# The level loop and the order of the grams in a chunked recurrence on one Trainium2 core

## The chip, the cores and the metric

The kernel runs on one core of a Trainium2 chip. The metric is the device time of one execution in microseconds (us). The kernel before took 4756.89 us in the median of three executions (4755.41 to 4758.74).

## The reference

Two blocks of layers follow each other; each has two layers. A layer of the first block mixes three kinds of heads over 256 context tokens and 1024 latent tokens: six heads of an RWKV-7 recurrence in both directions, six heads of grouped attention and four heads of windowed attention. The change lies in the recurrence alone. Per head, the state S is 64x64 and goes over the tokens one by one, forwards and backwards:

```python
def _rwkv7_step(S, inp):
    r, w, k, v, kk, b = inp
    sa = jnp.einsum('bhvk,bhk->bhv', S, kk)
    S = S * w[:, :, None, :] - sa[..., None] * b[:, :, None, :] + v[..., None] * k[:, :, None, :]
    return S, jnp.einsum('bhvk,bhk->bhv', S, r)
```

The backward direction runs the same step with the tokens reversed, and the outputs of both directions are added. Everything is in float32.

## The kernel before, in words

`rwkv_core` (from line 1606) runs the recurrence once per layer of the first block, so twice. It doesn't go token by token: the 1280 tokens are NB = 10 blocks of 128 tokens, each of two chunks c of 64, and the state is carried from chunk to chunk. The six heads are NP = 3 pairs g, each with two heads h, and two directions d; q = 2d + h counts the four of a pair. Most products are 64x64x64, one in a quarter of the systolic array: `half[0]` and `half[1]` are the lower and the upper 64 partitions, of the operands (a row half of the array) and of the result (a column half).

A block goes through these steps for each pair. TensorE's step is named first, then who takes the result from PSUM:

- `grams(b, g)` (line 1732): products of the loaded arrays of a chunk, masked by VectorE (`masked`, 2007) into G. They are made a block ahead, in the tail of block b - 1. The first array's gram is made in two products of 64 columns, since its two halves go to different column halves; the second's in one of 128. So a pair takes 24 products.
- `turned` (1748): eight transposes of loaded arrays, taken by ScalarE (X and V, 1967, 1968) and VectorE (2016).
- GpSimd masks the gram to the start matrix U0 and to the level matrices ML (2091, 2099); `start_t` (1765) makes the 64x64 inverse's start TU and its transpose; `bv` (1783) makes one more product.
- `state(b - 1, i)` (1882): the state's step for the block before, products at 1896 and 1904, additions at 2051 and 2056.
- Levels 1 to 5 double the size of the solved diagonal pieces: `level_w` (1797), copied by ScalarE to Ws (1980), then `level_d` (1816), which VectorE subtracts from both forms of TU in one instruction (2023). Levels 1 to 4 are four turns of a loop on TensorE, `pe.Fori(0, NL - 1)` at 1931. Level 5 is written out behind it: `level_w(b, NL, g)`, and `last_d` (1830) with half as many products, since only one form of TU is needed from there; VectorE subtracts it in two instructions of 64 partitions a pair (2027).
- `solve` (1843) multiplies TU with X; ScalarE takes the result to TX (1984). `outputs` (1854) makes four matrices a pair from TX, G and V, which VectorE adds and stores in QY and MN (2039, 2041). `state` needs them.

All orders are written by hand and every engine runs its own list; counters (semaphores) tie them together. TensorE's tail of a block is, before the change: loop, grams 0, W 0, W 1, grams 1, last_d 0, W 2, last_d 1, last_d 2, grams 2, solve 0, solve 1, outputs 0, solve 2, outputs 1, outputs 2 (lines 1940 to 1958). VectorE's: masks 0 and 1, the last level, mask 2, outputs 0, 1, 2. PSUM has eight banks, and the lists `d_at` to `state_at` (1668 to 1677) say which step writes which; a wait in `grams`, `turned`, `last_d` or `outputs` is for the step that had those banks before.

SP's queue (1690 to 1723) loads block b + 1 when the outputs of block b - 1 have been taken, and then stores the outputs of block b - 1. A load is six transfers of 384 KB (`rk_in`, one a pair and direction: 128 partitions, six arrays, 128 tokens, so runs of 512 bytes) and two of 192 KB for V. The first block's load stands first in the queue, six small constants behind it, the second block's load behind those. TensorE, VectorE and GpSimd all wait for the constants before they begin (1729, 2004, 2087).

The loop's body and the rest of TensorE's program are instructions read from memory; the profile shows their packets as the queue "q8 instruction".

Of the kernel before, what the change touches and what calls it, by code (L numbers as in the profile page):

```python
# [26 lines left out]
P = 128  # L27
# [6 lines left out]
HD = 64  # L34
# [1571 lines left out]
def rwkv_core(core):  # L1606
# [13 lines left out]
    d_in, v_in = [core.landing(f"rk_d{g}_loaded", per=2) for g in range(NP)], core.landing("rk_v_loaded", per=2)  # L1620
# [16 lines left out]
    with ExitStack() as s:  # L1637
# [32 lines left out]
        def w_at(g, last):  # L1670

            return bank[2 + g][:, 0:256] if g < 2 else bank[2][:, 0:256] if last else bank[0][:, 256:512]

        last_at, solve_at, bv_at = (bank[4], bank[5], bank[0]), (bank[2], bank[3], bank[2]), (bank[6], bank[7], bank[6])
        turned_at, start_at = (pair_at(0), pair_at(4), pair_at(0)), (by_chunk(2), by_chunk(6), by_chunk(2))
        gram_at, outputs_at = (pair_at(6), pair_at(0), pair_at(6)), (pair_at(0), pair_at(4), pair_at(6))
# [10 lines left out]
        with nc.Block() as block:  # L1687

            @block.sync
            def _(sp):  # L1690
                def load(b):
                    u, blk = b % 2, (b, back(b))
                    for g in range(NP):
                        for d in range(2):
                            sp.dma_start(D[:, u, g, d, 0:NA, :], T["CHK"][g * 2 + d, :, :, blk[d] * P:(blk[d] + 1) * P]
                                         .rearrange("w p t -> p w t")).then_inc(d_in[g].on(u), 16)
                        if g == 0:
                            for d in range(2):
                                sp.dma_start(VI[:, u, d, :, :], T["VT"][:, blk[d] * P:(blk[d] + 1) * P]
                                             .rearrange("(g p) t -> p g t", p=P)).then_inc(v_in.on(u), 16)  # L1700
# [25 lines left out]
            def _(pe):  # L1726
# [5 lines left out]
                def grams(b, g):  # L1732
# [5 lines left out]
                    elif b:  # L1738
                        pe.wait_ge(dl.sem, dl.nth(number(b - 1, NL - 1, 1 + g) + 1))
                    for d in range(2):  # L1740
                        for x, arr, a0, n in ((0, A_BH, A_KT, 1), (1, A_BH, A_RT, 1), (2, A_KH, A_KT, 2)):
                            for c, h in tiles:
                                rows, tok = half[h], half[c]
                                o = gram_at[g][h][half[1 - c if x == 0 else c], d * 256 + x * CH:d * 256 + (x + n) * CH]
                                ins = nc.tensor.matmul(o, D[rows, u, g, d, arr, tok], D[rows, u, g, d, a0:a0 + n, tok], start=True, stop=True)
                    ins.then_inc(pg.sem, 1)

                def turned(b, g):
# [3 lines left out]
                    if g < 2:  # L1752
                        after(pe, dq, NP * (b - 1) + g + 1)
# [29 lines left out]
                def bv(b, g):  # L1783
# [6 lines left out]
                    for q in range(4):  # L1790
                        d, h = q // 2, q % 2
                        for c in range(2):
                            ins = nc.tensor.matmul(bv_at[g][half[c], q * CH:(q + 1) * CH], G[half[c], u, g, d, h, 2, :],
# [1981 lines left out]
```

## Time and profile before

| | us |
|---|---|
| median of three runs | 4756.89 (4755.41 to 4758.74) |
| the profiled execution's own time | 4744.87 |
| its span (first to last instruction) | 4743.1 |
| TensorE busy, 86% of the span | 4102.1 |
| VectorE busy, 58% | 2756.3 |
| ScalarE busy, 33% | 1549.2 |
| GpSimd busy, 32% | 1498.3 |
| recurrence, first layer (from 556 to 978) | 422 |
| recurrence, second layer (from 2056 to 2475) | 419 |

PE is TensorE, DVE is VectorE, ACT is ScalarE, POOL is GpSimd, SP is SyncE. A float32 product of TensorE appears as two matmul records with a weight load each, so 24 products are 48 records; a transpose is one record. The brackets at the end of a timeline line give the time for which the engine stood just before, and what released it; "issue" means that it waited for nothing that the profile shows. Times in a timeline are from the start of the span.

### The profile page before, as it was taken

The page shows a single profiled execution, that of the slowest core. Times are in us where ns is not written, and L with a number is a line of the kernel's source. Part 1 is how long each engine was busy: PE and PEld are TensorE (multiplying, and loading weights), DVE is VectorE, ACT ScalarE, POOL GpSimd, SP SyncE. Part 2 cuts the span into 40 slices and gives each one's busy share as a digit, 9 for nine tenths or more (in the row PEclk, how much of TensorE's full clock was granted, in tenths as well). Part 3 has the DMA queues.
Part 4 walks back from the last instruction along what each step waited for, and adds up shares of the span by engine and source line. Part 5 has one row for each costly group of instructions (what it writes and reads, how often), then busy time and mean ns, then how long its engine had stood idle before and what let it go on. Part 6 is the DMA issues. An engine that isn't in the chain of part 4 may idle for free. (4 is left out here: it accounts for less than half of the span.)

```text
span 4743.1 us, 105248 instructions
## 1 busy us (share of the span) xinstructions
PE 4102.1 (86%) x43986; PEld 3151.5 (66%) x43986; DVE 2756.3 (58%) x4726; ACT 1549.2 (33%) x2721; POOL 1498.3 (32%) x1210
## 2 busy tenths in 40 slices
PE   6999888869989799888886999599679889978898
PEld 4878688836657587678874667488436677853566
DVE  3465455556657357545556665755657656557565
ACT  1333232325542133222224552200356420025542
POOL 2233143411004323324432013655132145514213
PEclk8999999979999899899998999699899999989899
DMA  6455533261235545643324134433312443340324
GB/s 195 154 176 190 167 83 83 60 219 33 62 93 173 156 152 202 201 118 83 83 79 123 46 78 168 149 111 104 122 35 66 126 163 100 104 142 7 83 64 175
DMA packets 502686, 560.45 MB, mean 118 GB/s; under 512 B 97532, under 2 KB 397084, under 8 KB 500180
## 3 DMA queue, kind: packets, MB, share of 16 engines
q1 hardware_dynamic: 374676, 475.93, 32.2%
q10 hardware_dynamic: 127616, 78.95, 5.7%
q8 instruction: 287, 4.70, 0.4%
q14 instruction: 107, 0.88, 0.1%
HBM read 366.75 MB, written 192.23 MB: 118 GB/s over the span
## 5 line engine op out<-in xcount | busy, mean ns | idle before, releaser
L1096 PE MATMUL pr_acc<-hH,pr_wh 128*128 128x512 f32 (+1 forms) x1288 | 482.4, 375 | 0.0
L1097 PE MATMUL pr_acc<-hL,pr_wh 128*128 128x512 f32 (+1 forms) x1288 | 466.1, 362 | 0.0
L1098 PE MATMUL pr_acc<-hH,pr_wl 128*128 128x512 f32 (+1 forms) x1288 | 465.6, 361 | 0.0
L2660 ACT ACTIVATE an_p<-an_p,an_stat 128x1280 f32<-128x1280 f32 (+5 forms) x372 | 339.7, 914 | 162.0 <-DVE an_stat L2738 156.5
L2600 PE MATMUL an_t<-ident,an_p 128*128 128x128 f32 x2152 | 318.5, 282 | 40.5 <-ACT an_pT L2667 28.1
L2600 PEld LDWEIGHTS an_t<-ident,an_p 128*128 128x128 f32 x2152 | 235.8, 141 | 164.1 <-issue 68.0
L2693 POOL TENSOR_TENSOR an_kl<-an_k,an_kh 128x1280 fp32r<-128x1280 f32 (+3 forms) x36 | 78.5, 2181 | 833.6 <-DVE an_qh L2718 833.6
L2734 DVE CUSTOM_DVE_ANT_0 an_p<-an_s,an_mask 128x256 f32<-128x256 f32 (+8 forms) x308 | 274.8, 892 | 99.5 <-PE an_s L2583 67.1
L2091 POOL TENSOR_TENSOR rk_ml<-rk_g,rk_lmask 128x256 f32<-128x256 f32 x300 | 210.7, 729 | 357.7 <-PE rk_ps L1812 357.0
L1465 POOL TENSOR_TENSOR sp_sl<-sp_w,sp_sh 128x512 fp32r<-128x512 f32 x172 | 246.0, 1437 | 196.4 <-DVE sp_sh L1540 177.9
L2625 PE MATMUL an_oacc<-an_pT,an_v 128*64 128x512 f32 (+3 forms) x1224 | 297.9, 561 | 4.0 <-DVE an_pT L2745 1.9
L1374 PE MATMUL sp_acc<-sp_ch,sp_sh 128*128 128x512 f32 x728 | 285.4, 392 | 7.6 <-POOL sp_sl L1465 7.6
L1140 POOL TENSOR_TENSOR pr_wl<-pr_w,pr_wh 128x1024 fp32r<-128x1024 f32 x58 | 142.7, 2461 | 472.2 <-DVE pr_wh L1160 472.2
L1376 PE MATMUL sp_acc<-sp_ch,sp_sl 128*128 128x512 f32 x728 | 284.8, 391 | 0.0
L1375 PE MATMUL sp_acc<-sp_cl,sp_sh 128*128 128x512 f32 x728 | 284.8, 391 | 0.0
L1096 PEld LDWEIGHTS pr_acc<-hH,pr_wh 128*128 128x128 f32 x1288 | 245.4, 191 | 58.0 <-issue 20.7
L2667 ACT COPY an_pT<-an_t 128x512 f32<-128x512 f32 (+3 forms) x356 | 186.0, 540 | 294.5 <-PE an_t L2600 293.6
L1097 PEld LDWEIGHTS pr_acc<-hL,pr_wh 128*128 128x128 f32 x1288 | 245.2, 190 | 37.8 <-issue 1.0
L1098 PEld LDWEIGHTS pr_acc<-hH,pr_wl 128*128 128x128 f32 x1288 | 244.8, 190 | 38.2
L2745 DVE COPY an_pT<-an_t 128x512 f32<-128x512 f32 (+3 forms) x256 | 155.6, 615 | 178.4 <-PE an_t L2600 175.7
L2023 DVE TENSOR_TENSOR rk_tu<-rk_tu,rk_ps 128x512 f32<-128x512 f32 x240 | 151.7, 683 | 183.6 <-PE rk_ps L1826 183.5
L2582 PE MATMUL an_s<-an_kh,an_qh 128*128 128x256 f32 (+2 forms) x564 | 198.3, 364 | 22.5 <-POOL an_qh L2697 13.5
(386 smaller groups left out, 10011.3 us busy)
## 6 DMA issues: line engine op xcount, KB each, us to landing
CHK<-ri_out SPq DMA_DIRECT2D x24, 1920.0 KB, 8.0
rk_in<-CHK SPq DMA_DIRECT2D x120, 384.0 KB, 6.5
pr_w<-in_w_in ACTq DMA_DIRECT2D x58, 512.0 KB, 3.9
UT<-pr_out SPq DMA_DIRECT2D x45, 640.0 KB, 4.3
sp_w<-in_w_in ACTq DMA_DIRECT2D x50, 512.0 KB, 5.1
U<-sp_c SPq DMA_DIRECT2D x100, 256.0 KB, 2.0
mod_w<-in_w_mod SPq DMA_DIRECT2D x16, 1024.0 KB, 7.9
mo_w<-in_w_out SPq DMA_DIRECT2D x16, 1024.0 KB, 10.2
```

The costliest lines, as they stand in the source:

```text
L1096: nc.tensor.matmul(out, wh[:, u, k, 0:m], hi, start=(k == 0), stop=False)
L1097: nc.tensor.matmul(out, wh[:, u, k, 0:m], lo, start=False, stop=False)
L1098: ins = nc.tensor.matmul(out, wl[:, u, k, 0:m], hi, start=False, stop=(k == KT - 1))
L1374: nc.tensor.matmul(to, sH[:, a, k, :], cH[:, i, k, :], start=(k == 0), stop=False)
L1375: nc.tensor.matmul(to, sH[:, a, k, :], cL[:, i, k, :], start=False, stop=False)
L1376: ins = nc.tensor.matmul(to, sL[:, a, k, :], cH[:, i, k, :], start=False, stop=(k == H - 1))
L1465: g.tensor_tensor(sL[:, slot(q, i)], weight(q, i), sH[:, slot(q, i)], ALU.subtract).then_inc(w_lo.sem, 1)
L2091: return nc.gpsimd.tensor_tensor(out, G[:, b % 2, g, :, :, 0, :], lm[:, :, lv:lv + 1, :].to_broadcast([P, 2, 2, CH]), ALU.mult)
L2600: ins = nc.tensor.transpose(bank[:, j * P:(j + 1) * P], Pm[:, n % NPM, j, col:col + P], ident[:])
L2625: ins = nc.tensor.matmul(O[half * HD:(half + 1) * HD, cs], V[:, c % 2, blocks[n][k], :], PT[:, buffer(n, k), cs], start=(p == 0), stop=(p ...
L2660: nc.scalar.activation(row, row, ACT.Exp, bias=stat[:, n % NPM, j, 1:2], scale=heads[groups[n][0]].scale, accum_out=total[:, n % 4, j:j + ...
L2734: V_.tensor_tensor_reduce(out=Pm[:, n % NPM, j, 0:width], in0=scores_at(m, width), in1=extra, scale=1.0, scalar=-3.0e38, op0=ALU.add, op1= ...
```

## The change

Four things change, all in `rwkv_core`.

1. Level 5 becomes a fifth turn of TensorE's loop, like the others, and `last_d` goes. VectorE subtracts it in one instruction a pair instead of two.
2. The order of the tail is new. TensorE: loop, solve 0, solve 1, grams 0, solve 2, outputs 0, grams 1, grams 2, outputs 1, outputs 2. VectorE: last level, mask 0, outputs 0, mask 1, mask 2, outputs 1, outputs 2. Banks and waits follow: outputs 0 use banks 4 and 5, outputs 1 use banks 0 and 1 and wait for mask 1, outputs 2 wait for mask 2; the next block's first transposes wait for outputs 1 instead of outputs 0, its second for outputs 0.
3. The first array's gram is one product of 128 columns, so a pair takes 16 products. All grams now lie in the other chunk's half of the partitions.
4. For that, the arrays that meet the grams later are loaded with their chunks exchanged. A load of a pair and direction is four transfers instead of one: two of two whole arrays, and two that bring half of the tokens of two arrays, in runs of 256 bytes. V comes in four transfers instead of two, also in runs of 256 bytes. A block's load is 28 transfers instead of 8.

```diff
@@ loads
-                            sp.dma_start(D[:, u, g, d, 0:NA, :], T["CHK"][g * 2 + d, :, :, blk[d] * P:(blk[d] + 1) * P]
-                                         .rearrange("w p t -> p w t")).then_inc(d_in[g].on(u), 16)
+                            src = T["CHK"][g * 2 + d, :, :, blk[d] * P:(blk[d] + 1) * P].rearrange("w p t -> p w t")
+                            for a in (A_BH, A_KT):
+                                sp.dma_start(D[:, u, g, d, a:a + 2, :], src[:, a:a + 2, :]).then_inc(d_in[g].on(u), 16)
+                            for c in range(2):
+                                sp.dma_start(D[:, u, g, d, A_BE:A_BE + 2, half[1 - c]], src[:, A_BE:A_BE + 2, half[c]]) \
+                                    .then_inc(d_in[g].on(u), 16)
                         if g == 0:
                             for d in range(2):
-                                sp.dma_start(VI[:, u, d, :, :], T["VT"][:, blk[d] * P:(blk[d] + 1) * P]
-                                             .rearrange("(g p) t -> p g t", p=P)).then_inc(v_in.on(u), 16)
+                                for c in range(2):
+                                    t0 = blk[d] * P + c * CH
+                                    sp.dma_start(VI[:, u, d, :, half[1 - c]], T["VT"][:, t0:t0 + CH].rearrange("(g p) t -> p g t", p=P)) \
+                                        .then_inc(v_in.on(u), 16)
@@ grams
-                        for x, arr, a0, n in ((0, A_BH, A_KT, 1), (1, A_BH, A_RT, 1), (2, A_KH, A_KT, 2)):
+                        for x, arr in ((0, A_BH), (2, A_KH)):
                             for c, h in tiles:
                                 rows, tok = half[h], half[c]
-                                o = gram_at[g][h][half[1 - c if x == 0 else c], d * 256 + x * CH:d * 256 + (x + n) * CH]
-                                ins = nc.tensor.matmul(o, D[rows, u, g, d, arr, tok], D[rows, u, g, d, a0:a0 + n, tok], start=True, stop=True)
+                                o = gram_at[g][h][half[1 - c], d * 256 + x * CH:d * 256 + (x + 2) * CH]
+                                ins = nc.tensor.matmul(o, D[rows, u, g, d, arr, tok], D[rows, u, g, d, A_KT:A_KT + 2, tok], start=True, stop=True)
@@ TensorE, tail of a block
-                    with pe.Fori(0, NL - 1) as i:
+                    with pe.Fori(0, NL) as i:
...
+                    solve(b, 0)
+                    solve(b, 1)
                     if more:
                         grams(b + 1, 0)
-                    level_w(b, NL, 0)
-                    level_w(b, NL, 1)
+                    solve(b, 2)
+                    outputs(b, 0)
                     if more:
                         grams(b + 1, 1)
-                    last_d(b, 0)
-                    level_w(b, NL, 2)
-                    last_d(b, 1)
-                    last_d(b, 2)
-                    if more:
                         grams(b + 1, 2)
-
-                    solve(b, 0)
-                    solve(b, 1)
-                    outputs(b, 0)
-                    solve(b, 2)
                     outputs(b, 1)
                     outputs(b, 2)
@@ VectorE
-                    for lv in range(1, NL):
+                    for lv in range(1, NLEV):
...
                     if more:
                         masked(b + 1, 0)
+                    outputs(b, 0)
+                    if more:
                         masked(b + 1, 1)
-                    level(b, NL, 0)
-                    level(b, NL, 1)
-                    level(b, NL, 2)
-                    if more:
                         masked(b + 1, 2)
-                    for g in range(NP):
-                        outputs(b, g)
+                    outputs(b, 1)
+                    outputs(b, 2)
```

In `bv`, `solve` and `outputs` the halves of the operands or of the result are exchanged to match; their numbers and shapes of products stay.

## Rows read from the trace of the kernel before

**Rows 1.** Windows, first recurrence: length; busy PE, PEld, DVE, ACT, POOL; PEclk, DMA share, GB/s.

```profile
556.00:978.00 422.00, 362.67 (x13700) 341.70 (x13700) 226.49 (x433) 121.80 (x300) 167.41 (x250) 0.97 0.31 79
```

**Rows 2.** Timeline of TensorE, a block's tail: start, us, engine, line, operation, count [idle].

```profile
757.89 1.13 PE L1745 MATMUL rk_ps<-rk_in 64*64 64x64 f32 x48 [0.59 <-DVE rk_tu L2023]
...
763.76 0.49 PE L1850 MATMUL rk_ps<-rk_x,rk_tu 64*64 64x128 f32 x5
...
765.52 0.45 PE L1866 MATMUL rk_ps<-rk_g,rk_tx 64*64 64x128 f32 x8
...
766.94 0.94 PE L1850 MATMUL rk_ps<-rk_x,rk_tu 64*64 64x128 f32 x12
...
771.48 0.44 PE L1760 MATMUL rk_ps<-ident,rk_in 128*128 128x128 f32 x2
```

**Rows 3.** Timeline of VectorE in the same tail.

```profile
759.11 1.29 DVE L2010 TENSOR_TENSOR rk_g<-rk_ps,rk_mask 128x512 f32<-128x512 f32 x2 [0.77 <-PE rk_ps L1745]
...
762.14 2.61 DVE L2027 TENSOR_TENSOR rk_tu<-rk_tu,rk_ps 64x256 f32<-64x256 f32 x6
...
767.28 0.43 DVE L2039 TENSOR_TENSOR rk_qy<-rk_ps,rk_in 128x256 f32<-128x256 f32 x1 [1.21 <-PE rk_ps L1878]
...
768.28 0.41 DVE L2041 TENSOR_TENSOR rk_mn<-rk_ps,rk_dg 128x256 f32<-128x256 f32 x1
```

**Rows 4.** Timeline of TensorE, third and fourth turn of the loop.

```profile
751.02 1.56 PE L1812 MATMUL rk_ps<-rk_tu,rk_ml 64*64 64x64 f32 x46 [0.27 <-issue]
...
754.29 1.56 PE L1812 MATMUL rk_ps<-rk_tu,rk_ml 64*64 64x64 f32 x46 [0.26 <-issue]
```

**Rows 5.** Timeline of TensorE in a layer's last block: fourth turn, first solve.

```profile
956.01 1.56 PE L1812 MATMUL rk_ps<-rk_tu,rk_ml 64*64 64x64 f32 x46 [0.26 <-issue]
...
962.12 0.61 PE L1850 MATMUL rk_ps<-rk_x,rk_tu 64*64 64x128 f32 x8
```

**Rows 6.** Timeline of TensorE, pauses of one block before and during the load.

```profile
723.65 0.27 PE L1869 MATMUL rk_ps<-rk_g,rk_tx 64*64 64x64 f32 x1 [0.23 <-issue]
...
727.07 0.27 PE L1866 MATMUL rk_ps<-rk_g,rk_tx 64*64 64x128 f32 x1 [0.39 <-issue]
...
736.05 0.38 PE L1896 MATMUL rk_ps<-rk_h,rk_mn 64*64 64x64 f32 x5 [0.72 <-issue]
...
742.38 2.47 PE L1812 MATMUL rk_ps<-rk_tu,rk_ml 64*64 64x64 f32 x46 [2.45 <-issue]
```

**Rows 7.** DMA queues: packets, MB, share, from 715 to 731, 731 to 744, 1244 to 1248.

```profile
q8 instruction: 4, 0.07, 1.7%
...
q1 hardware_dynamic: 6280, 3.14, 89.0%
q8 instruction: 2, 0.03, 1.0%
...
DMA packets 84, 0.02 MB, mean 5 GB/s; under 512 B 83, under 2 KB 83, under 8 KB 84
q1 hardware_dynamic: 84, 0.02, 2.3%
```

**Rows 8.** Windows, as rows 1, the microsecond after the longest pause.

```profile
743.00:744.00 1.00, 1.00 (x24) 1.00 (x22) 0.00 (x0) 0.37 (x1) 0.67 (x1) 0.50 0.22 62
```

**Rows 9.** Timelines of SP's queue and of TensorE at the start of a layer.

```profile
556.47 0.96 SPq L1695 DMA_DIRECT2D rk_in<-CHK  x2
...
563.03 1.28 SPq L1709 DMA_DIRECT2D rk_pair<-in_pair  x1
564.35 0.43 SPq L1711 DMA_DIRECT2D rk_mask<-in_mask_gram  x1
...
570.35 4.95 PE L1745 MATMUL rk_ps<-rk_in 64*64 64x64 f32 x128 [6.67 <-issue]
```

**Rows 10.** Timeline of SP's queue, the load inside a block.

```profile
730.76 0.95 SPq L1695 DMA_DIRECT2D rk_in<-CHK  x2
...
732.87 5.94 SPq L1695 DMA_DIRECT2D rk_in<-CHK  x4
```

More of the change, by code:

```diff
@@ L1619, in rwkv_core @@
     PER = NL * NP
-    d_in, v_in = [core.landing(f"rk_d{g}_loaded", per=2) for g in range(NP)], core.landing("rk_v_loaded", per=2)
+    d_in, v_in = [core.landing(f"rk_d{g}_loaded", per=8) for g in range(NP)], core.landing("rk_v_loaded", per=4)
     stored = core.landing("rk_y_stored", per=2)
@@ L1752, in turned @@
                     if g < 2:
-                        after(pe, dq, NP * (b - 1) + g + 1)
+                        after(pe, dq, NP * (b - 1) + 2 - g)
                     else:
@@ L1801, in level_w @@
                     pe.wait_ge(dl.sem, dl.nth(k - NP + 1))
-                    last = isinstance(lv, int)
-                    if g == 2 and not last:
+                    if g == 2:
                         after(pe, dh, 2 * b)
                         after(pe, dy, 2 * b)
-                    if not last:
-                        pe.sem_inc(turn.sem, 1)
+                    pe.sem_inc(turn.sem, 1)
                     for q in range(4):
@@ L1811, in level_w @@
                             far = half[1 - c]
-                            ins = nc.tensor.matmul(w_at(g, last)[half[c], q * CH:(q + 1) * CH], ML[far, g, d, h, :], TU[far, g, c, q, :],
+                            ins = nc.tensor.matmul(w_at[g][half[c], q * CH:(q + 1) * CH], ML[far, g, d, h, :], TU[far, g, c, q, :],
                                                    start=True, stop=True)
@@ L1828, in level_d @@
                     ins.then_inc(pd.sem, 1)
-                def last_d(b, g):
-                    k = number(b, NL, g)
-                    pe.wait_ge(aw.sem, aw.nth(k + 1))
-                    if g == 2 and b + 1 < NB:
-                        pe.wait_ge(dm.sem, dm.nth(NP * (b + 1) + 2))
-                    elif g == 2:
-                        pe.wait_ge(dl.sem, dl.nth(number(b, NL - 1, 2) + 1))
-                    for q in range(4):
-                        for c in range(2):
-                            ins = nc.tensor.matmul(last_at[g][half[c], q * CH:(q + 1) * CH], Ws[half[c], g, q, :], TU[half[c], g, c, q, :],
-                                                   start=True, stop=True)
-                    ins.then_inc(pd.sem, 1)
                 def solve(b, g):
```

45 lines of the change are left out of this document (20 added, 25 removed).

## The prediction

> **What bounds the kernel now.** The page has TensorE busiest, and its chain says little here, so I went by stage. The changed code is the recurrence, which runs once in each of two layers; the first run takes about 422 us, TensorE is busy in 362.67 us of that and VectorE in 226.49 [rows 1]. So what counts is TensorE's own order of work plus every place where it stands. The timeline of one block's tail shows them. From the first gram of the next block to the first transpose it takes 771.48 - 757.89 = 13.59 us; grams of one pair take 0.93 us (0.89 us in the shape after the change, below), solves of two pairs 765.52 - 763.76 = 1.76, so 0.88 each, and the outputs of one pair 766.94 - 765.52 = 1.42 [rows 2]. VectorE's part of it: two masks 1.29 us, six half subtractions 2.61, and the four additions of one pair 1.41, from 767.28 to 768.69 [rows 3]. A turn of the level loop takes 754.29 - 751.02 = 3.27 us [rows 4].
>
> Two other things bound it. TensorE's instructions come in packets of 16 KB on a queue of their own. Between loads four came in 16 us; while the next block was loading only two came in 13 us [rows 7]. The pauses marked "issue" fall in step: 0.23 and 0.39 us, 3.42 us apart, before the load; 0.72 and 2.45 us, 6.33 us apart, in it [rows 6]. After the longest, the granted clock is 0.50, the 1.2 GHz level [rows 8]. And each layer's first gram starts at 570.35, some 14 us after the first load was issued at 556.47, because it waits for constants that stand behind the load on SP's queue [rows 9].
>
> **The change, part by part.** Of the 20 blocks (ten per layer), 18 have a next block.
>
> *The fifth turn.* It costs 3.27 us and takes out the written-out last level: 24 W and 24 D products of a block. In a last block, where no grams stand between, that level alone can be read: from the fourth turn's start, 956.01, to the first solve, 962.12, is 6.11 us [rows 5]. After the change the same stretch is 3.27 plus the last turn up to the first solve, about 3.25: 6.5. Plus 0.4 us for each of two last blocks: +1 us.
>
> *The first grams in one product.* 24 products a pair become 16, but the columns stay: two 64-wide ones become one 128-wide. The unit was 0.93 us for 512 columns in each quarter of the array. A solve unit also moves 512 columns in a row, in 128-wide products, in 0.88 us, so I take 0.89. The gain is 0.04 x 54 units = 2 us, inside the next term.
>
> *The new order of the tail.* I count from the moment where the first gram started before, 3.60 us after the last turn's start (757.89 less 754.29). The first solve needs only the last level's first subtraction and can go at about -0.3. Then solve, solve, grams, solve (to 3.2), outputs 0 (to 4.6), grams, grams (to 6.4). Outputs 1 now wait for the mask of pair 1, which on VectorE stands behind the additions of outputs 0: those run 5.0 to 6.3, the mask to 7.6, so TensorE stands for 1.2 us. Outputs 1 and 2 then end at 10.5. The next block's first transposes use the banks of outputs 1, which are free at 10.9: 0.4 us more. Sum 3.27 + 10.9 = 14.2 against 13.59, so +0.6 a block and 18 x 0.6 = +11 us. Without the two standstills it would be 14.2 - 1.6 = 12.6 (-18 us over 18 blocks); with the small pauses for instructions that the tail has now and a slower way out of the loop, up to 14.9 (+23). I take the middle, since each wait in it is one that VectorE's rows give. The fifth wide subtraction is shorter in sum than the six halves, and the queue behind it on VectorE is the mask. ScalarE's copies and GpSimd's masks lie beside.
>
> *The loads.* A block's 8 transfers become 28: 12 of two arrays, 12 of half chunks and 4 for V. Runs of 512 bytes fall from 5376 to 3072, and 4608 runs of 256 bytes come. In the load the queue moved 6280 packets in 13 us at 89%: 29.5 ns of an engine for each. The nearest row with short packets has 84 in 4 us at 2.3%: 17.5 ns [rows 7]. So the data take between (3072 x 29.5 + 4608 x 17.5) / 16 = 10.7 us and 7680 x 29.5 / 16 = 14.2 us, against 9.9. SP needs 0.43 us and a gap of 0.05 for a small transfer [rows 9], so 28 x 0.48 = 13.4 us against 8.05 in a block (730.76 to 738.81, [rows 10]). They land some 12 us before the grams need them, so no gram waits. But the stretch in which instruction packets are slow grows from 12 to about 15 us, thinner. It may slow one packet more (5.5 less 3.6 us, +1.9 a block) or each less (-1 a block); I take +0.3 x 16 blocks that load = +5 us, ends -16 and +30.
>
> The Trainium skill (DMA: Bandwidth & Descriptors, Specifications) says that a transfer below 512 bytes misses line rate and becomes a read-modify-write. By that rule the upper end, 14.2 us, holds, and the window of slow packets is at its longest; the short row above speaks against it.
>
> *The start of a layer.* The constants stand behind the first load. SP takes 563.03 - 556.47 = 6.56 us for its 8 transfers [rows 9]; 28 take 13.4, or 11.3 if each takes 0.40. So +4.8 to +9 us a layer, and I take 6.5: +13 us for two. Nothing covers it: all engines wait for these constants. The second load then lies further over the first block: +1 us a layer, +2.
>
> The sum is 1 + 11 + 5 + 13 + 2 = +32 us. The profiled execution itself took 4744.87 us (its span 4743.1), so 4776.9; the median of the three runs, 4756.89, lies 12.0 above it, which gives **4789**.
>
> **The rivals.** *Instructions bound the straight part (faster).* Per block 72 products go from the straight code, each two loads and two multiplies: 288 instructions, 1.13 packets. If TensorE really went at the packets' pace there, the block would change by 3.27 - 1.13 F, F being the time of a packet. With 16 us to pay elsewhere this turns to a gain from F = 3.7; between 3.5 (no load) and 5.5 (load) at F = 4.6 it gives -1.9 x 18 = -34, +16, so 4738. For it: every pause beside a load is of this kind. Against: the packets removed belong to the tail, where the pauses are 0.2 to 0.45 us. The Trainium skill (Runtime: NRT & Kernel Launch, Instruction fetch mechanics) gives TensorE a buffer of 2048 instructions filled in 16 KB blocks and calls the fetching mostly hidden. By that rule this rival would be worth nothing; the trace disagrees with it, with 2.45 us for one pause.
>
> *One more slow packet in each block (slower).* If the longer load reaches past the first turn of the loop, which it does from about 15.5 us on, 16 x 1.9 = 30 in place of 5: 4814. It is the other end of the load term.
>
> *The standstills of the tail are not there, and the start costs its lower end.* Then -18 + 10 + 8 = 0: 4757, no change. It would need the masks to be early. That the one product saves nothing at all is inside the forecast.
>
> **How the numbers follow.** Forecast 0.52, its own range 4771 to 4807; one more slow packet 0.2; instructions bound 0.2; nothing 0.08. A difference of 0.2% (9.5 us) is about what a measurement can tell here. Faster takes most of the chance of the rival of the instructions, 0.18; same takes its rest, the case of no change and a little of the forecast, 0.12; slower 0.70. The range 4742 to 4822 covers all but the far ends of the bounds (4733 and 4833).
>
> **What would show it.** In the profile after: the first gram of a layer 6 to 7 us later after the first load; five turns of 3.3 us; TensorE standing before the outputs of pair 1 for about 1.2 us, released by VectorE's mask; 28 loads a block, the busy stretch about 15 us; issue pauses in state and first turn summing to what they were, near 3 us a block. I am wrong if blocks get shorter than 40 us on average, if no wait stands before outputs 1, or if the load stretch hardly grows.

## The result and the profile after

The changed kernel takes **4726.4 us** (median of four, 4722.1 to 4733.3) against 4756.3 for the kernel before on the same chip: ratio 0.9934, interval 0.9919 to 0.995. The forecast was 4789, slower; it is faster, below the range's low end of 4742. The profiled execution took 4722.17 us, its span 4720.0.

The page after: totals of each engine, and the DMA queues (packets, MB, share).

```profile
span 4720.0 us, 105768 instructions
PE 4091.5 (87%) x43986; PEld 3144.1 (67%) x43986; DVE 2738.4 (58%) x4666; ACT 1553.0 (33%) x2721; POOL 1499.3 (32%) x1210
q1 hardware_dynamic: 427156, 475.95, 32.5%
q8 instruction: 264, 4.33, 0.4%
```

The same queue of instructions on the page of before:

```profile
q8 instruction: 287, 4.70, 0.4%
```

TensorE's busy time is 11 us less, and the instructions come in 23 packets of 16 KB fewer.

The first recurrence after, in the window of [rows 1]:

```profile
556.00:978.00 422.00, 361.46 (x13720) 341.06 (x13720) 219.49 (x407) 123.89 (x303) 167.10 (x250) 0.96 0.33 83
```

TensorE's work is nearly the same, but the stage no longer fills the window. From its first warm-up products to those of the next stage the two recurrences take 410.8 and 407.3 us, before 421.8 and 419.0: **-22.7 us** together, which is all of the -22.7 between the two profiled executions.

A block runs from its first transpose to the next block's. The first transposes of blocks 1 and 9 of the first layer, before and then after:

```profile
610.52 0.44 PE L1760 MATMUL rk_ps<-ident,rk_in 128*128 128x128 f32 x2
937.04 0.44 PE L1760 MATMUL rk_ps<-ident,rk_in 128*128 128x128 f32 x2
```

```profile
617.48 0.41 PE L1763 MATMUL rk_ps<-ident,rk_in 128*128 128x128 f32 x2 [0.25 <-DVE rk_mn L2017]
925.95 0.41 PE L1763 MATMUL rk_ps<-ident,rk_in 128*128 128x128 f32 x2 [0.25 <-DVE rk_mn L2017]
```

A block took 326.52 / 8 = 40.8 us and takes 308.47 / 8 = 38.6 (second layer 40.5 and 38.2). The gain is there, and nowhere else:

| where | forecast | measured |
|---|---|---|
| start of a layer, two | +13 | +12 |
| first block of a layer, two | +3 | -0.6 |
| blocks 1 to 8 of a layer, 16 | +15 | **-36** |
| last blocks and the rest | +1 | +2 |

(The forecast's +11 for 18 tails is spread here at 0.6 each.) Within a middle block the gain lies ahead of the loop, not in the tail. The table takes the means of the 16 middle blocks in the two profiled executions, in us; the tail is taken from the start of the loop's fourth turn, since the kernel before has no fifth.

| part of a block | before | after | change |
|---|---|---|---|
| first transpose to first W | 10.98 | 8.97 | -2.01 |
| first W to fourth turn | 12.14 | 11.47 | -0.67 |
| fourth turn to next first transpose | 17.51 | 17.92 | +0.41 |

Who kept TensorE waiting in the first recurrence, in the view of the waits (line waited for, releaser: us in total, times, longest). Before:

```profile
PE rk_ps L1812 <- issue: 13.7, 33, 2.5
PE rk_ps L1745 <- issue: 7.0, 2, 6.7
...
PE rk_ps L1824 <- issue: 4.8, 4, 2.2
PE rk_ps L1826 <- issue: 4.4, 3, 1.9
PE rk_ps L1896 <- issue: 4.3, 4, 2.2
...
PE rk_ps L1793 <- issue: 1.7, 1, 1.7
...
PE rk_ps L1904 <- issue: 1.5, 2, 1.0
```

After:

```profile
PE rk_ps L1748 <- DMA rk_ec<-EC: 13.5, 1, 13.5
PE rk_ps L1814 <- issue: 11.3, 42, 0.4
PE rk_ps L1856 <- DVE rk_g L1992: 10.6, 9, 1.2
PE rk_ps L1826 <- issue: 7.9, 5, 2.1
...
PE rk_ps L1828 <- issue: 1.1, 1, 1.1
```

Two things are to be seen. The wait before the outputs of pair 1 came as forecast: nine times 1.2 us, released by VectorE's mask. And the pauses *ahead of* the level loop are gone: at the state's products (before L1896 and L1904), at L1793 and at the first W of a block. L1812 had pauses up to 2.5 us; its counterpart L1814 has none over 0.4 in this layer (one of 0.7 in the second), and 42 times 0.27 are the loop's own turns. The pauses inside the first turn (before L1824 and L1826, after L1826 and L1828) are still there: 9.2 and 9.0 us.

That such a pause is a wait for instructions shows in the packet records of the traces. Over the middle blocks of all 17 traces TensorE makes 334 pauses of more than 0.7 us marked "issue", and every one ends 1.1 to 2.0 us after an instruction packet of 16 KB has landed; in the first layer only 12 to 16% of all moments lie 1.1 to 1.9 us behind such a landing. The pauses of the first turn are no exception. The longest pause of before [rows 6] ends at 742.38. The last packet ahead of it, in the DMA view from 739.4 to 739.5:

```profile
q8 instruction: 1, 0.02, 65.5%
```

65.5% of 16 engines for 0.1 us is 1.05 us, so this packet landed at about 740.5. Its own transfer was not slow: the one ahead of a pause of 1.97 us in b_short_loads, where hardly any load runs, took 1.12 us. What gets longer beside a dense load is the time from one packet's start to the next's, so the delay arises before a packet is moved, and of that the traces have no record.

### The profile page after: what moved, and what is told of

Its sections match the earlier page's. It is cut to its first block and busy times, and to the rows that moved or that the text cites. A ratio compares the mean times of both kernels' runs of the same rounds, so it can differ in the third digit from the quotient of the medians.

```text
span 4720.0 us, 105768 instructions
## 1 busy us (share of the span) xinstructions
PE 4091.5 (87%) x43986; PEld 3144.1 (67%) x43986; DVE 2738.4 (58%) x4666; ACT 1553.0 (33%) x2721; POOL 1499.3 (32%) x1210
## 5 line engine op out<-in xcount | busy, mean ns | idle before, releaser
L2004 DVE TENSOR_TENSOR rk_tu<-rk_tu,rk_ps 128x512 f32<-128x512 f32 x300 | 188.8, 682 | 190.5 <-PE rk_ps L1828 190.5
```

## The experiments

Two parts of the change could have done it: the loads, or TensorE's shorter code. Every edit is on top of one of the two kernels, named first. *Block* is the mean of the 16 middle blocks, from first transpose to first transpose; *ahead* is its part up to the first W; both are from one profiled execution, so that 0.3 us of a block says little. A profiled execution can also lie well off its kernel's median: that of before took 4744.9 us against 4756.3, that of b_split_loads 4734.6 against 4727.5, that of b_short_loads 4724.4 against 4714.0, that of after 4722.2 against 4726.4. So where a share is counted, both reckonings are given below. Ratios are to the kernel before on the same chip, with a 95% interval; no run but a_whole_loads has one that reaches 1.

| run | median us | ratio | block | ahead |
|---|---|---|---|---|
| before | 4756.3 | 1 | 40.63 | 10.98 |
| after | 4726.4 | 0.9934 (0.9919 to 0.995) | 38.36 | 8.97 |
| b_split_loads | 4727.5 | 0.9946 (0.993 to 0.9963) | 39.17 | 9.57 |
| a_whole_loads | 4749.0 | 0.9995 (0.9981 to 1.0009) | 40.54 | 10.06 |
| b_pair_loads | 4731.2 | 0.9947 (0.9926 to 0.9968) | 38.97 | 9.68 |
| b_short_runs | 4749.7 | 0.9977 (0.9964 to 0.9989) | 40.96 | 10.44 |
| b_short_loads | 4714.0 | 0.9917 (0.9901 to 0.9934) | 38.41 | 9.53 |
| a_short_loads | 4712.8 | 0.9925 (0.9908 to 0.9941) | 37.38 | 8.82 |
| b_late_loads | 4711.5 | 0.9909 (0.9891 to 0.9928) | 38.33 | 9.50 |
| a_late_loads | 4715.7 | 0.9914 (0.9898 to 0.9931) | 37.84 | 8.83 |
| a_fifth_straight | 4747.1 | 0.9976 (0.9967 to 0.9986) | 39.26 | 8.97 |
| a_three_grams | 4746.4 | 0.9975 (0.9962 to 0.9987) | 39.23 | 9.02 |
| a_same_quarters | 4728.8 | 0.9934 (0.9916 to 0.9952) | 38.62 | 9.29 |
| a_new_tail | 4711.5 | 0.9904 (0.9882 to 0.9925) | 37.68 | 9.27 |
| a_constants_first | 4723.5 | 0.9941 (0.9922 to 0.9959) | 38.17 | 9.01 |
| b_late_constants | 4709.8 | 0.9896 (0.9878 to 0.9914) | 38.42 | 9.47 |
| a_best | 4697.7 | 0.9881 (0.9861 to 0.99) | 37.11 | 9.04 |

### The loads alone, and all but the loads

b_split_loads: the kernel before with the loads in 28 transfers, each chunk to its old place.

```diff
-                            sp.dma_start(D[:, u, g, d, 0:NA, :], ...)
+                            for a in (A_BH, A_KT):
+                                sp.dma_start(D[:, u, g, d, a:a + 2, :], src[:, a:a + 2, :]).then_inc(d_in[g].on(u), 16)
+                            for c in range(2):
+                                sp.dma_start(D[:, u, g, d, A_BE:A_BE + 2, half[c]], src[:, A_BE:A_BE + 2, half[c]]) \
...
```

> The kernel before with only its block loads cut into 28 transfers as in the change (same bytes, runs of 256 bytes where the change has them, chunks not exchanged); TensorE's program is that of before. Theory A (the small transfers keep the DMA queues thinner, so instruction packets come sooner during a load): the stretch from the first transpose to the first W of a block falls from 11.0 us to about 9.0 on average; 16 x 2.0 = 32 us less, 12 us more for the two starts, so about 4736. Theory B (fewer instructions outside the loop are what saved the time): that stretch stays near 11 us, and the starts cost 12 us: about 4768.

a_whole_loads is the reverse: the kernel after with the eight transfers of before (lines 1695 and 1699 of before's code in place of the 28, so the chunks are not exchanged).

> The changed kernel with its block loads as the 8 whole transfers of before; the chunks are then not exchanged, so the values differ from the reference's, the work is the same. Theory A: the stretch from the first transpose to the first W goes back from 9.0 us to about 11, +32 us, less 12 us for the starts: about 4746. Theory B: it stays at 9.0 us and the starts save 12 us: about 4714.

With before's code the split takes 1.46 us off a block (40.63 to 39.17), with after's 2.18 (40.54 to 38.36). All else of the change together, with whole loads, gives 0.09 a block and no measurable time. The medians put the loads' share higher: ratio 0.9946 for the split loads is -25.7 us, and less the 12 us that the starts cost it is -38 us, or 2.4 a block; with after's code (0.9995 to 0.9934) it is 2.6. SP's first and last issue of one load in b_split_loads, in the timeline of its queue:

```profile
734.63 0.87 SPq L1697 DMA_DIRECT2D rk_in<-CHK  x2
...
750.51 0.98 SPq L1699 DMA_DIRECT2D rk_in<-CHK  x2
```

The DMA queues in the same load, from 735 to 748:

```profile
q1 hardware_dynamic: 5893, 1.95, 59.7%
q8 instruction: 3, 0.05, 1.5%
```

SP takes 16.9 us for the 28 issues, and the 16 DMA engines stay 40% free, where they moved the same load at 89% before [rows 7]. In the waits of its first recurrence the W products (L1818 here) have no long pause any more, where L1812 had 2.5 us:

```profile
PE rk_ps L1818 <- issue: 8.5, 31, 0.6
```

In a_whole_loads, with the whole loads under after's code, such pauses are back, at V products (`bv`, L1791) and at W (L1808), by TensorE's timeline:

```profile
706.03 0.96 PE L1808 MATMUL rk_ps<-rk_tu,rk_ml 64*64 64x64 f32 x16 [1.47 <-issue]
...
743.18 0.45 PE L1791 MATMUL rk_ps<-rk_v,rk_g 64*64 64x64 f32 x8 [1.45 <-issue]
```

So it is the load's form that makes the pauses ahead of the loop come and go. The packet records give the size of it, as the mean time from one instruction packet's start to the next's, over the packets that start ahead of the loop in a middle block: 5.0 us in before and 4.8 in a_whole_loads, but 3.9 in b_split_loads and 4.1 in after.

### Is it the size of a transfer, or the length of its runs?

b_pair_loads: before, 24 transfers, all with runs of 512 bytes. b_short_runs: before, the six large transfers cut in two by chunk, so 12 large ones with runs of 256 bytes, and the two of V as they were.

```diff
+                            for a in range(0, NA, 2):
+                                sp.dma_start(D[:, u, g, d, a:a + 2, :], src[:, a:a + 2, :]).then_inc(d_in[g].on(u), 16)
...
+                                for v in range(NP):
+                                    sp.dma_start(VI[:, u, d, v, :], T["VT"][v * P:(v + 1) * P, blk[d] * P:(blk[d] + 1) * P]).then_inc(v_in.on(u), 16)
```

```diff
+                            for c in range(2):
+                                sp.dma_start(D[:, u, g, d, 0:NA, half[c]], src[:, :, half[c]]).then_inc(d_in[g].on(u), 16)
```

> The kernel before with its block loads cut into 24 transfers (two arrays, or one pair of V, each), all in runs of 512 bytes: many small transfers, no short runs. Theory A1 (what helps is that small transfers follow each other at SP's pace and leave the DMA engines gaps): the first transpose to the first W takes 9.6 us as with the split loads, the starts cost 10 us: about 4728. Theory A2 (what helps are the short runs, between which an instruction packet gets through sooner): it stays at 11 us, about 4766.

> The kernel before with each of its six block transfers cut in two by chunk, so all their runs are 256 bytes, and V as before: 14 larger transfers, short runs. A1: the DMA engines are as full as before, the stretch stays at 11 us, the starts cost some us: about 4762. A2: the stretch falls to 9.6 us: about 4738.

The queue of transfers during a load, b_pair_loads from 734.5 to 747.5:

```profile
q1 hardware_dynamic: 4356, 2.08, 57.7%
```

b_short_runs from 738 to 751:

```profile
q1 hardware_dynamic: 9973, 2.70, 98.6%
```

Many small transfers with long runs give the gain of the split loads (0.9947 and 0.9946); few large ones with short runs keep the queue at 98.6% and give less than half of it (0.9977). Their profiled block is no shorter than before's (40.96), which doesn't fit the ratio of 0.9977; the stretch ahead of the loop is, at 10.44 against 10.98. From one instruction packet's start to the next's it takes 4.7 us in b_short_runs and 4.1 in b_pair_loads. What counts most is the number of pieces in which SP hands the load out, and with it the rate; no run separates the size of a transfer from that rate, and a small part for the short runs isn't ruled out.

### Without the load, and with the load elsewhere

b_short_loads and a_short_loads cut the loads of blocks 2 to 9 to 16 of 128 partitions in each kernel.

```diff
-                    u, blk = b % 2, (b, back(b))
+                    u, blk, n = b % 2, (b, back(b)), P if b < 2 else 16
...
+                            sp.dma_start(D[0:n, u, g, d, 0:NA, :], ...
```

> The kernel before with the loads of blocks 2 to 9 cut to 16 of 128 partitions (an eighth of the bytes; these blocks compute on old data). It prices all that a load costs TensorE. Both theories: the first transpose to the first W takes 9.1 us and the first turn 3.3 in every block, as in the last block, which has no load beside it: 16 x 3.2 = 51 us less, about 4705.

> The changed kernel with the loads of blocks 2 to 9 cut in the same way, still 28 transfers. Theory A: without any traffic the change should be a loss, 0.4 us a block for the fifth turn and the new tail (18 blocks: 7 us) and 12 us for the starts, so 19 us above the same cut of the kernel before: about 4724. Theory B: the instructions saved count without loads too, so it is at or below that cut: 4705 or less.

Without the load's traffic before's code gains 2.2 us a block, and the change's code is then worth 38.41 - 37.38 = 1.03 a block. By the medians it is less: 1.2 us between the two runs and 10.5 us of later starts make 11.7, or 0.7 a block. The 4714 missed what was expected: the pauses of the first turn stay (1.97 us at 741.58), about 1 us a block with no load beside them. So this part of the pauses, which I had put down to the load too, isn't the load's. They are waits for an instruction packet all the same: the one at 741.58 follows the landing of a packet by 1.32 us. A warning on counting packets: in this run a window of 13 us in the same place has two instruction packets as well, at 16.9% of load traffic and with no pause ahead of the loop. Counts by themselves don't show lateness; the pauses do, and the time between packets' starts, 3.9 us here.

b_late_loads moves the load on SP's queue behind the first W of the loop, and behind the store.

```diff
-                    if b and b + 1 < NB:
-                        sp.wait_ge(dq.sem, dq.nth(NP * b))
-                        load(b + 1)
                     if b:
                         store(b - 1)
+                    if b and b + 1 < NB:
+                        sp.wait_ge(pw.sem, pw.nth(number(b, 1, NP - 1) + 1))
+                        load(b + 1)
```

> The kernel before with one thing moved: SP issues the load of block b + 1 only after the W products of the first turn of block b's loop, and the store of block b - 1 ahead of it. Theory A (a load in flight delays the packets of instructions): in the loop none are needed, so the pauses of the straight part and of the first turn go, 3 us a block: 16 x 3 = 48 us less, about 4705, and no gram waits for data. Rival (the pauses come from entering the loop and from the amount of code, not from the load): unchanged, 4755.

> The changed kernel with its load moved in the same way. Theory A: what its thinner load still costs, 1.0 us a block by the run with short loads, goes: 16 us less, about 4711. Rival: the 15 us that its 28 transfers take now reach the grams, and these wait: no gain or a loss.

b_late_loads keeps the eight large transfers and before's TensorE code, and takes **4711.5 us**, 15 less than the whole change (the intervals of the two ratios overlap a little: 0.9891 to 0.9928 and 0.9919 to 0.995). The DMA queues from 701 to 714, where SP issued the load from 699.51 on:

```profile
q1 hardware_dynamic: 5426, 2.71, 81.9%
q8 instruction: 1, 0.02, 0.6%
```

A pause of TensorE in the first turn of the next block's loop, in its timeline:

```profile
739.94 0.27 PE L1824 MATMUL rk_ps<-rk_ws,rk_tu 64*64 64x64 f32 x2 [1.95 <-issue]
```

The load runs now while TensorE repeats the loop's code, and one instruction packet comes in those 13 us. The traffic is as dense as ever (81.9% of a window whose last 3 us lie behind the load's end); it only no longer meets the stretch in which TensorE needs new code. On top of the change the same move (a_late_loads, 4715.7) gives 0.52 a block.

### TensorE's code

a_fifth_straight: after, the fifth level written out behind a loop of four (288 more instructions of TensorE per block outside the loop, the same products in the same order).

```diff
-                    with pe.Fori(0, NL) as i:
+                    with pe.Fori(0, NL - 1) as i:
...
+                    for g in range(NP):
+                        level_w(b, NL, g)
+                    for g in range(NP):
+                        level_d(b, NL, g)
```

> The changed kernel with the same fifth level written out behind a loop of four turns: the same products in the same order, 288 more instructions a block outside the loop. If the instructions outside the loop count (each 1.13 packets more a block), pauses of 1 to 2 us a block come back, 18 to 36 us: about 4750. If only the shape of the loads counts, nothing moves: 4727.

a_three_grams: after, the first array's gram in two products of 64 columns again (96 more instructions per block).

```diff
-                        for x, arr in ((0, A_BH), (2, A_KH)):
+                        for x, arr, a0, n in ((0, A_BH, A_KT, 1), (1, A_BH, A_RT, 1), (2, A_KH, A_KT, 2)):
```

> The changed kernel with the first array's gram in two products of 64 columns again, to the same half: 24 products a pair, 96 instructions a block more, same columns. By the run with the fifth level written out, 288 instructions cost 0.9 us a block, so these should cost 0.3 us: 5 us in the recurrence, about 4732. If the columns alone count: 4727.

Both cost the same: +0.90 and +0.87 a block, 4747.1 and 4746.4, some 20 us. The products are those of after in both; only the number of instructions outside the loop grows. The gram units of a_three_grams take 2.02 us for two pairs where after takes 1.96, and then the pause comes. Two rows of its timeline, then a pause in the written-out level of a_fifth_straight:

```profile
690.44 2.02 PE L1748 MATMUL rk_ps<-rk_in 64*64 64x64 f32 x95
...
697.64 0.34 PE L1865 MATMUL rk_ps<-rk_v,rk_g 64*64 64x64 f32 x8 [1.31 <-issue]
```

```profile
714.73 0.27 PE L1826 MATMUL rk_ps<-rk_ws,rk_tu 64*64 64x64 f32 x1 [2.33 <-issue]
```

The pauses for instructions over 0.33 us of a tail sum to 1.6 and 1.0 us in the two layers of a_fifth_straight and to 1.0 and 0.9 in a_three_grams, against 0.42 and 0.43 in after. That 96 instructions cost as much as 288 missed my expectation of +0.3. One reading is that the fifth level brings 3.28 us of work with its 288 instructions, so that work covers most of its packet, while the extra gram products bring none. No run tells that reading from others. Nor does the amount of code alone set the price. a_fifth_straight and b_split_loads both fetch 287 instruction packets where after fetches 264, and both have its loads in 28 transfers; the first is some 20 us slower than after, the second 1 us by its median and 6 by its ratio. So the place of the code counts as well, and no run varies it by itself.

a_same_quarters: after, V products and solves write to the half of the array that before used, so that neighbouring units no longer lie in different quarters.

```diff
-                            ins = nc.tensor.matmul(bv_at[g][half[c], q * CH:(q + 1) * CH], G[far, ...
+                            ins = nc.tensor.matmul(bv_at[g][far, q * CH:(q + 1) * CH], G[far, ...
...
-                            ins = nc.tensor.matmul(solve_at[g][half[1 - c], q * P:(q + 1) * P], TU[half[c], ...
+                            ins = nc.tensor.matmul(solve_at[g][half[c], q * P:(q + 1) * P], TU[half[c], ...
```

> The changed kernel with the results of bv and of solve written to the half of their own operand's partitions, so that both work in the same two quarters of the array as state and outputs next to them, as before the change (the values land in the wrong half). Theory C: the change also won because neighbouring groups of products now lie in other quarters and overlap: the unpaused stretch from the first transpose to the first W goes from 8.65 back to 9.09 us and the tail grows by 0.3: 14 us more, about 4740. Rival: quarters don't matter, 4727.

Ahead of the loop the undisturbed blocks took 9.09 us before, 8.65 after and 9.05 here: so the exchange of the halves does shorten this stretch, by 0.4 us. The timelines show how: V products (L1797) in after begin among the outputs' products,

```profile
815.86 0.69 PE L1894 MATMUL rk_ps<-rk_qy,rk_h 64*64 64x64 f32 x18
816.35 0.27 PE L1797 MATMUL rk_ps<-rk_v,rk_g 64*64 64x64 f32 x2
```

and in a_same_quarters behind them, one group after the other:

```profile
816.55 0.87 PE L1894 MATMUL rk_ps<-rk_qy,rk_h 64*64 64x64 f32 x24
817.25 0.63 PE L1797 MATMUL rk_ps<-rk_v,rk_g 64*64 64x64 f32 x16
```

A block is 0.26 longer and the time no different (4728.8 against 4726.4).

a_new_tail: after, with the standstill before outputs 1 taken out: TensorE goes solve, grams, solve, grams, solve, grams, then all outputs; VectorE does the three masks first.

```diff
                     solve(b, 0)
-                    solve(b, 1)
                     if more:
                         grams(b + 1, 0)
-                    solve(b, 2)
-                    outputs(b, 0)
+                    solve(b, 1)
...
+                    for g in range(NP if more else 0):
+                        masked(b + 1, g)
+                    for g in range(NP):
+                        outputs(b, g)
```

> The changed kernel with grams 0, 1, 2 behind solve 0, 1, 2 and the outputs last, and VectorE's three masks ahead of its outputs. The standstill of 1.2 us before outputs 1 and the short one before the next transposes should go: by VectorE's rows the tail would be 1.4 us shorter, 18 x 1.4 = 25 us, about 4702. Rival: the packets of instructions become the bound (3 packets at 3.5 us against 9.5 us of work), half of it is lost: about 4712. Rival 2: VectorE is only late elsewhere and nothing is gained: 4727.

VectorE's wait at L1856 is gone from the view of the waits, which in after held 10.6 us; of what is left:

```profile
PE rk_ps L1814 <- issue: 12.1, 41, 1.2
...
PE rk_ps L1856 <- issue: 3.8, 6, 1.2
```

A block is 0.68 us shorter, 4711.5: of the 1.45 us (1.20 and 0.25) which the two standstills hold in after, less than half. The tail itself, from the fourth turn on, is 1.16 shorter (17.92 to 16.76), but the rest of the block gives 0.47 back. The part ahead of the loop went from 8.97 to 9.27, and L1814 shows a pause of 1.2 again: the tail is done sooner, and instructions are late in the next stretch.

### The start of a layer, and the best of both

a_constants_first: after, the six constants issued ahead of the first load. b_late_constants: before, with that and the late loads. a_best: after, with late loads, new tail and constants first.

```diff
-                load(0)
                 sp.dma_start(pair[:], T["pair"]).then_inc(cst.sem, 16)
...
                 sp.dma_start(ec[:], T["EC"].rearrange("g p d c -> p g d c")).then_inc(cst.sem, 16)
+                load(0)
                 load(1)
```

> The changed kernel with the six constants issued ahead of the first block's load. The first gram should start some 10 us earlier after the layer's start, but grams 2 still need the last of the 28 transfers, so the first transpose gains 4 to 5 us a layer: 9 us in both, about 4718.

> The kernel before with late loads and the constants ahead of the first load. Late loads alone gave 4711; in the profile of the changed kernel the constants ahead took the start of both layers 5 to 6 us down for 28 transfers, with 8 they should give 3 us a layer: about 4705.

> The changed kernel with late loads, the new tail and the constants first together. The late loads gave 11 us against the changed kernel, the constants should give 9, the tail 14 to 25: about 4685, below both kernels and below the kernel before with late loads (4711).

The start of a layer after (SP's first issue and the first constant's, TensorE's first gram), and then in a_constants_first:

```profile
558.53 0.88 SPq L1694 DMA_DIRECT2D rk_in<-CHK  x2
...
572.86 0.47 SPq L1712 DMA_DIRECT2D rk_pair<-in_pair  x1
...
578.32 1.98 PE L1748 MATMUL rk_ps<-rk_in 64*64 64x128 f32 x32 [13.48 <-DMA rk_ec<-EC]
```

```profile
557.22 0.33 SPq L1711 DMA_DIRECT2D rk_pair<-in_pair  x1
...
566.43 1.10 PE L1748 MATMUL rk_ps<-rk_in 64*64 64x128 f32 x32 [1.92 <-DMA rk_in<-CHK]
```

The first gram comes at 566.43 instead of 578.32, 11 us sooner in each layer, but the two recurrences lose only 1.6 and 5.8 us of their 410.8 and 407.3, and the time 3 us, which is inside the intervals: what follows then waits for the arrays of the second and third pair, and the part ahead of the first block's loop takes 8.5 and 8.2 us instead of 6.7. The clock has a share in that: from 570 to 583 the granted clock is 0.50, the 1.2 GHz level, so that the first transposes run at it, while in after it is back at 1.00 when they start, at 583.50. With before's code the gain over b_late_loads is 1.7 us, inside the intervals. a_best, **4697.7 us**, is the fastest version run: 58 us below before and 29 below the change, though above the 4685 that I expected from adding up the single gains.

## Why the prediction was wrong

**The start of a layer** held: +13 forecast, +12 measured. The constants were issued 572.86 - 558.53 = 14.3 us after the first load instead of 6.6, and the first gram of a layer came 5.9 and 6.2 us later.

**The tail's own order** held. Where no pause disturbs it, the fourth turn takes 3.28 us and the stretch from the fifth turn's start to the next block's first transpose 14.18, 17.46 in all, where before's undisturbed tails take about 17.0 from the fourth turn's start: +0.4, with +0.6 forecast. With all pauses in, the means differ by as much (17.51 and 17.92). The standstill of 1.2 us is in each of nine tails, and the small wait at the next block's transposes in six of them, 0.25 us instead of 0.4. Rows of one tail, TensorE's then VectorE's:

```profile
688.43 1.96 PE L1748 MATMUL rk_ps<-rk_in 64*64 64x128 f32 x63
...
691.59 0.45 PE L1856 MATMUL rk_ps<-rk_g,rk_tx 64*64 64x128 f32 x8 [1.20 <-DVE rk_g L1992]
...
694.80 0.41 PE L1763 MATMUL rk_ps<-ident,rk_in 128*128 128x128 f32 x2 [0.25 <-DVE rk_mn L2017]
```

```profile
688.83 0.42 DVE L2015 TENSOR_TENSOR rk_qy<-rk_ps,rk_in 128x256 f32<-128x256 f32 x1 [1.09 <-PE rk_ps L1868]
...
690.16 2.47 DVE L1992 TENSOR_TENSOR rk_g<-rk_ps,rk_mask 128x512 f32<-128x512 f32 x4
```

So the rival in which the standstills are not there fell: they are, and the time came out lower all the same.

**The first step that failed is the loads term.** I took +0.3 us for each of 16 blocks (bounds -1 and +1.9); split loads measure -1.5 with before's code and -2.2 with after's by the blocks, -2.4 and -2.6 by the medians, beyond even the low bound. I had read rightly that the load stretch grows and gets thinner: its traffic is at 57.6% where it was 89%. For after, the queue of transfers from 659 to 672, in a load that SP issues from 658.90 to 676.22:

```profile
q1 hardware_dynamic: 5696, 1.90, 57.6%
```

But I weighed the longer stretch above the thinner one. The runs show the opposite: a load at 58 to 60% for 17 us takes nearly all pauses ahead of the loop away, one at 89 to 99% makes them. The rival "one more slow packet" was the same error carried further, since the stretch did reach past the first turn. The term's prices were too coarse as well: 3.6 and 5.5 us for a packet stand in no row, and the traces have 3.9 us from packet to packet without a load, 5.0 beside the dense one and 3.9 to 4.1 beside the thin ones.

The Trainium skill (DMA: Bandwidth & Descriptors, Specifications) says that transfers below 512 bytes miss line rate. By packets little of it is seen here: 16 x 13 us x 57.6% / 5696 = 21.0 ns for after's mix of long and short, 20.6 for b_short_runs, 27.6 for b_pair_loads, 29.5 before. With 29.5 for a long one that makes 15 to 20 ns for a short one (60% of the packets in after, 92% in b_short_runs): more than half the price for half the bytes, so a lower rate, but less than a long one's. The load's data, 7680 x 21.0 / 16 = 10.1 us, took less than my 10.7 to 14.2. The same page's rule to batch transfers to 1 MiB or more (section Bandwidth) would speak against 28 small ones. For a load in this place the small ones are better, because not the load is waited for but the instructions that are fetched beside it; put elsewhere, the large ones do as well or better (b_late_loads).

**The second is what the sum left out: the code ahead of the loop.** It had no term for that stretch but the loads. The exchanged halves shorten it by 0.4 us a block, which I had not costed at all; the V products stand in no term of the sum. On top of that come fewer pauses, though not under whole loads. By the blocks the change's code gives -1.03 without load traffic, -0.81 under split loads and -0.09 under whole ones; by the medians -0.7, -0.1 to -0.4 and about -0.1. All of the -0.81 and of the -1.03 lies ahead of the loop (-0.60 and -0.71) and in its first three turns (-0.38 and -0.51), while the tail is 0.2 longer in both. The rival "instructions bound the straight part", to which I gave 0.2, foresaw a gain of this kind: 3.27 - 1.13 F a block, and F of 3.6 to 3.8 would fit the first two. But its 4738 lies near the measured time by luck: it took the gain from slow packets beside an unchanged load, where the whole-loads run shows none. My argument against it was that the packets removed belong to the tail with pauses of 0.2 to 0.45 us. That was read from one tail; over 16 blocks the tail's pauses for instructions over 0.33 us were 0.68 us each, and fall to 0.42. Where I went by the nearest row a mean over blocks was to be had.

The Trainium skill (Runtime: NRT & Kernel Launch, Instruction fetch mechanics) calls fetching mostly hidden. The prediction already had the trace against it, and a_three_grams puts a size on it: 0.9 us a block for code that adds no columns of work.

In sum over the 16 blocks, by the profiled blocks: split loads with before's code -23, code on top of them -13, together the -36 of the table. By the medians it is -38 and -1 to -6. Either way the loads are the larger part, and the exact share of the code stays open. "Blocks shorter than 40 us on average" was named as what would show me wrong, and did; the pauses for instructions over 0.33 us, which I expected to stay near 3 us a block, went from 3.7 to 1.6.

**What stays open**: the pauses inside the loop's first turn, about 1 us a block. They outlive the missing load, the late load and the shorter code. Each of those over 0.7 us ends 1.1 to 1.7 us after an instruction packet has landed, so they are waits for code; why the packet is late there with no load beside it, no run tests. Open is also what holds a packet back beside a dense load, since its own transfer is hardly longer.

## What to carry to other kernels

Where an engine runs long straight code, ask of each bulk transfer which code is being fetched beside it: put the load beside a loop that is already running, or let the issuing queue hand it out in small pieces, before touching the engine's work. Here the first alone was worth 44 us of 4755, with no change to what any compute engine does. And when pauses are cured one at a time, don't count on getting all of it: here the new tail gave back about half, as what ended sooner met late instructions in the next stretch.

## What the runs showed of the hardware

- Instruction packets are late beside dense transfers: at 89% and 98.6% of the 16 DMA engines TensorE pauses for up to 2.5 us ahead of the loop, at 57.6 to 59.7% for 0.9 us at most there in the first recurrence, though the transfers move the same bytes. The packets start 4.7 to 5.0 us apart beside the dense loads, 3.9 to 4.1 beside the thin ones and 3.8 to 3.9 with hardly any traffic.
- The transfer of an instruction packet is hardly longer beside a load: in before a median of 1.18 us for the 29 with traffic over 80% around them, 0.96 for the 74 with under 5%.
- TensorE goes on 1.1 to 2.0 us after the packet has landed, in all 334 pauses over 0.7 us.
- A small transfer costs SP about 0.5 us at the start of a layer and 0.6 in a block (17.3 us for 28), which goes with the thinner traffic: 57.6% for the same load.
- Unit groups of TensorE that lie in different quarters of the array overlap at their border: the stretch ahead of the loop is 8.65 us with the exchange and 9.05 without. The Trainium skill (TensorEngine Tiling (Array Packing), Key Properties) says that different tiles can load weights and multiply in parallel; the rows at 815.86 and 816.35 agree.
- A pause can cost clock, but not each long one does. In after, TensorE stands for 1.86 us before 745.61, and then the granted clock is 0.50, the 1.2 GHz level, where it stayed at 1.00 after the pause of 1.10 us that ended at 669.19, and after one of 2.12 us that ended at 631.50. Windows of after, columns as in [rows 1]:

```profile
671.00:672.00 1.00, 1.00 (x40) 1.00 (x37) 0.57 (x1) 0.44 (x2) 0.49 (x1) 1.00 0.84 224
...
748.00:749.00 1.00, 1.00 (x27) 1.00 (x26) 0.00 (x0) 0.37 (x1) 0.87 (x2) 0.50 0.60 139
```
